# Modulation weights read by TensorE in fp32 as they land, in four column tiles, with the first loads and the DFT put in another order

## The reference, cut to what matters

```
sh_a, sc_a, g_a, sh_m, sc_m, g_m = split(silu(c) @ mod_w[i] + mod_b[i], 6)      # mod_w[i]: 1024 x 6144
h = modulate(x, norm_mix_g[i], sh_a, sc_a)                                      # norm, scale, shift
x = x + g_a * mixer(h)                       # Fourier, differential attention, MLA, Fourier
x = x + g_m * sq_relu_mlp(modulate(x, norm_mlp_g[i], sh_m, sc_m), w1, w2)       # 1024 -> 4096 -> 1024
```

## Time and profile before

| | |
|---|---|
| median of 3 runs | 3569.93 us (3569.45 to 3571.2) |
| the profiled execution | 3565.45 us |
| its span, first to last instruction | 3564.2 us |
| mean granted TensorE clock | 0.956 |
| busy: PE, DVE, ACT, POOL | 3267.6, 1996.8, 1624.1, 1341.1 us |
| moved | 460.01 MB, mean 129 GB/s |

### The profile page before, as it was taken

How to read it: one execution, slowest core, us unless ns; L and a number is a source line. 1 busy time by engine, 2 the same in 40 slices (tenths; PEclk the granted TensorE clock), 3 DMA queues, 4 the chain that set the end, 5 groups by cost and what they waited for, 6 DMA issues and landing times.

```text
span 3564.2 us, 51196 instructions
## 1 busy us (share of the span) xinstructions
PE 3267.6 (92%) x21038; PEld 2848.7 (80%) x21038; DVE 1996.8 (56%) x3159; ACT 1624.1 (46%) x2532; POOL 1341.1 (38%) x542
## 2 busy tenths in 40 slices
PE   4989999897678999979998898999999999999899
PEld 3868888785557888756898897787899987878899
DVE  5465544428855555366665664656546646664565
ACT  4454333325444333355544444555444445555443
POOL 4343344224432444401344333243353442434434
PEclk7999999997779999989999999999999999999999
DMA  6344444322322444411453454233355542434454
GB/s 201 118 130 154 154 154 143 106 83 95 118 95 83 151 148 150 138 42 36 155 189 116 154 179 128 86 107 96 107 168 161 172 133 85 118 95 136 150 179 152
DMA packets 469159, 460.01 MB, mean 129 GB/s; under 512 B 8896, under 2 KB 467520, under 8 KB 468928
## 3 DMA queue, kind: packets, MB, share of 16 engines
q1 hardware_dynamic: 465760, 453.32, 39.9%
q10 hardware_dynamic: 3168, 3.42, 0.3%
HBM read 455.66 MB, written 1.05 MB: 128 GB/s over the span
## 4 chain that ended last, share of the span: by engine, by line
PE 74%; DVE 13%; ACT 7%; issue 3%; POOL 2%; ACTq 0%; DMA 0%; DVEq 0%; POOLq 0%; SPq 0%
PE bank L341 21%; PE bank L342 20%; PE bank L343 20%; ACT wh L289 3%; DVE wl L304 2%; PE bank L382 2%; PE bank L383 2%; POOL wl L316 1%; DVE de L1187 1%; DVE sm L1174 1%; POOL sq L451 1%; PE bank L1328 1%; DVE hl L644 1%; PE bank L1319 1%; DVE sm L1172 1%
## 5 line engine op out<-in xcount | busy, mean ns | idle before, releaser
L316 POOL TENSOR_TENSOR wl<-raw,wh 128x768 fp32r<-128x768 f32 (+4 forms) x432 | 1212.2, 2812 | 2073.9 <-ACT wh L289 2073.9
L289 ACT ACTIVATE wh<-raw 128x2048 fp32r<-128x2048 f32 (+2 forms) x432 | 818.9, 1896 | 474.5 <-PE bank L343 450.3
L304 DVE TENSOR_TENSOR wl<-raw,wh 128x1280 fp32r<-128x1280 f32 (+2 forms) x408 | 679.2, 1665 | 452.3 <-ACT wh L289 451.9
L341 PE MATMUL bank<-nh,wh 128*128 128x272 f32 (+1 forms) x1712 | 510.1, 298 | 23.4 <-DVE nl L1651 22.8
L341 PE MATMUL bank<-xh,wh 128*128 128x512 f32 (+2 forms) x1312 | 462.1, 352 | 45.3 <-ACT xh L499 33.4
L343 PE MATMUL bank<-nh,wl 128*128 128x272 f32 (+1 forms) x1712 | 497.4, 291 | 0.0
L342 PE MATMUL bank<-nl,wh 128*128 128x272 f32 (+1 forms) x1712 | 496.1, 290 | 0.0
L342 PE MATMUL bank<-xl,wh 128*128 128x512 f32 (+2 forms) x1312 | 455.3, 347 | 0.0
L343 PE MATMUL bank<-xh,wl 128*128 128x512 f32 (+2 forms) x1312 | 454.6, 347 | 0.0
L341 PEld LDWEIGHTS bank<-nh,wh 128*128 128x128 f32 x1712 | 330.4, 193 | 40.0 <-issue 37.8
L341 PE MATMUL bank<-hh,wh 128*128 128x512 f32 (+1 forms) x1024 | 348.9, 341 | 3.5 <-DVE X L551 1.9
(11 more groups left out here) (397 smaller groups left out, 6209.2 us busy)
## 6 DMA issues: line engine op xcount, KB each, us to landing
raw<-in_mlp_w SPq DMA_DIRECT2D x128, 1024.0 KB, 5.4
raw<-in_mod_w SPq DMA_DIRECT2D x96, 1024.0 KB, 5.2
raw<-in_w_in SPq DMA_DIRECT2D x60, 1024.0 KB, 5.2
raw<-in_w_mlp_up SPq DMA_DIRECT2D x32, 1024.0 KB, 5.7
raw<-in_w_mlp_down SPq DMA_DIRECT2D x32, 1024.0 KB, 5.1
raw<-in_w_in SPq DMA_DIRECT2D x34, 512.0 KB, 4.6
raw<-in_w_ssd_down SPq DMA_DIRECT2D x16, 1024.0 KB, 5.3
raw<-in_diff_w_qkv SPq DMA_DIRECT2D x12, 1024.0 KB, 5.1
```

The source lines that it names most:

```text
L289: nc.scalar.activation(self.wtile(self.wh, c1), self.wtile(self.raw, c1), AF.Copy).then_inc(*up("act_wh", ("wh", c1)))
L304: nc.vector.tensor_tensor(l, r, h.bitcast(F32), ALU.subtract).then_inc(*up("dve_wl", ("wl_dve", c1)))
L316: nc.gpsimd.tensor_tensor(l, r, h.bitcast(F32), ALU.subtract).then_inc(*up("pool_wl", ("wl_pool", c1)))
L341: nc.tensor.matmul(o, ah, bh, start=first, stop=False)
```

## The change

Modulation chunks are not split any more. TensorE waits for the raw chunk itself and reads it as the moving operand of true fp32 matmuls; `cst` has 32 columns (two used), and row tile k goes into column tile k % 4, output partitions 32 (k % 4) onward, so that eight products with two rounds per column tile make a chunk. Two chunks (even and odd i) share a bank; the copy into `mrow`, the turn and the addition are done once for both. The turn is four fp32 matmuls with `mrow` (128x128) as stationary and `sel` (two columns that add up the four column tiles) as moving operand; VectorE adds once. The banks are 6 and 7 in place of the ring.

Since a modulation chunk stays in `raw` until TensorE has used it, a load waits for `used` of the chunk three before it where that is a modulation chunk. `wh` and `wl` slots and the look-ahead of three now count only the other chunks (`dense`, `nth`). At the start, five more raw buffers lie where `wh` and `wl` will be (EARLY = 8), and four chunks are loaded ahead of the DFT table. The first sum of squares is made by ScalarE and eight matmuls, without GpSimd. The 12 chunks of the Fourier layer are used inside the DFT loop, two behind each of the steps 1 to 6. In the attention two chunks are done behind each even unit, 0 to 22.

```
 def chunks(a):
...
-                if L == 0 and j < 3:
-                    mods(0, 8 + 4 * j, 12 + 4 * j)
+                if L == 0:
+                    mods(0, *((8, 14), (14, 16), (16, 18), (18, 20))[j])
...
-            mods(2, 0, 24, 0)
+            mods(2, 0, 24)
...
     def sp_load(self, upto):
-            if c >= RAWS:
-                SP.wait_ge(*at("wh", c - RAWS))
-                SP.wait_ge(*at("wl_dve", c - RAWS))
-                SP.wait_ge(*at("wl_pool", c - RAWS))
+            if c >= EARLY:
+                prev = c - EARLY if c < EARLY + RAWS else c - RAWS
+                if prev in self.nth:
+                    SP.wait_ge(*at("wh", prev))
+                    SP.wait_ge(*at("wl_dve", prev))
+                    SP.wait_ge(*at("wl_pool", prev))
+                else:
+                    SP.wait_ge(*at("used", prev))
...
+    def split_upto(self, c, ahead):
+        return min(self.nth[c] + ahead, len(self.dense))
+
-    def act_split(self, c):
-        while self.n_act <= min(c + SLOTS - 1, len(self.P) - 1):
-            c1 = self.n_act
+    def act_split(self, c, ahead=SLOTS):
+        while self.n_act < self.split_upto(c, ahead):
+            d, c1 = self.n_act, self.dense[self.n_act]
             ACT.wait_ge(*at("raw", c1))
-            if c1 >= SLOTS:
-                ACT.wait_ge(*at("used", c1 - SLOTS))
+            if d >= SLOTS:
+                ACT.wait_ge(*at("used", self.dense[d - SLOTS]))
+            else:
+                ACT.wait_ge(*at("used", RAWS + 2 * d))
...
-    def pe_mod(self, c, of=RING):
+    def pe_mod(self, c, rows=(6,), cols=(7,)):
-        h, l = self.pe_take(c)
+        PE.wait_ge(*at("raw", c))
         PE.wait_ge(*at("cst"))
-        b = self.pe_bank(of, "mod", L, i)
+        w = self.rawtile(c).rearrange("p (k n) -> p k n", k=8)
+        b = self.place["mod", L, i // 2] if i % 2 else self.pe_bank(rows, "mod", L, i // 2)
         for k in range(8):
-            nc.tensor.matmul(b[:, 0:256], self.cst[:, k, :], h[:, k, :], start=(k == 0), stop=False)
-            ins = nc.tensor.matmul(b[:, 0:256], self.cst[:, k, :], l[:, k, :], start=False, stop=(k == 7))
-        ins.then_inc(*up("pe_acc", ("acc", "mod", L, i), ("used", c)))
-        self.pe_turn()
-        self.turning = L, i, of
+            q = 32 * (k % 4)
+            ins = nc.tensor.matmul(b[q:q + 32, 256 * (i % 2):256 * (i % 2) + 256], self.cst[:, k, :], w[:, k, :], start=(k < 4), stop=(k >= 4))
+        ins.then_inc(*up("pe_acc", ("acc", "mod", L, i // 2), ("used", c)))
+        if i % 2:
+            self.turning = L, i // 2, cols
...
     def pe_turn(self):
-        for u in range(2):
-            ins = nc.tensor.transpose(b[:, 4 * u:4 * u + 4], r[0:4, 128 * u:128 * u + 128], self.ident[0:4, 0:4])
+        for u in range(4):
+            ins = nc.tensor.matmul(b[:, 2 * u:2 * u + 2], self.mrow[h % 2][:, 128 * u:128 * u + 128], self.sel[:], start=True, stop=True)
...
     def act_mod(self, c):
+        if i % 2 == 0:
+            return
+        nc.scalar.activation(self.mrow[h % 2][:], self.place["mod", L, h][:], AF.Copy).then_inc(*up("act_row", ("row", L, h), ("out", "mod", L, h)))
...
     def act_mlp(self, st, T, xs=None, nxt=None):
-            self.act_split(c)
             if p[0] == "mod":
                 self.act_mod(c)
                 c += 1
                 continue
+            self.act_split(c)
...
     def pe_fourier(self, L, S):
+            if L == 0 and 1 <= n <= 6:
+                self.pe_turn()
+                for i in (6 + 2 * n, 7 + 2 * n):
+                    self.pe_mod(self.ix["mod", 0, i])
+        self.pe_turn()
...
     def act_fourier(self, L, S):
+            if L == 0 and 1 <= n <= 6:
+                self.act_mod(self.ix["mod", 0, 7 + 2 * n])
+                if n >= 4:
+                    self.act_split(self.ix["fw", L, n - 4], 1)
...
     def pe_diff(self):
-            if mods and (n > 12 or n in (0, 2, 4, 6, 8, 10, 12)):
+            if mods and n >= 0 and n % 2 == 0:
+                self.pe_mod(mods.pop(0), (7,))
                 self.pe_mod(mods.pop(0), (7,))
...
     def sp(self):
-        self.sp_load(1)
+        self.sp_load(3)
         self.sp_dft(0)
```

More of the change, by code:

```diff
@@ L29 @@
 SLOTS = 3
+EARLY = 8
 RING = (0, 1, 2, 3)
@@ L114, in w, with mods @@
         out.append((name, w3(ap, r0, kt, c0, n), kt, n, share))
-    def mods(layer, lo, hi, share=5):
+    def mods(layer, lo, hi):
         for i in range(lo, hi):
-            w(("mod", layer, i), a["mod_w"][layer], 0, 8, 256 * i, 256, share)
+            w(("mod", layer, i), a["mod_w"][layer], 0, 8, 256 * i, 256)
     mods(0, 0, 8)
@@ L191, in __init__ @@
         self.ix = {p[0]: c for c, p in enumerate(self.P)}
+        self.dense = [c for c, p in enumerate(self.P) if p[0][0] != "mod"]
+        self.nth = {c: d for d, c in enumerate(self.dense)}
         self.loaded = self.n_act = self.n_dve = self.n_pool = 0
@@ L215, in memory @@
         self.wl = [self.mem(f"wl{i}", 2048, F32R, b + 16384 * i + 8192) for i in range(SLOTS)]
+        self.early = [self.mem(f"early{i}", 2048, F32, b + 8192 * i) for i in range(EARLY - RAWS)]
         b += 16384 * SLOTS
@@ L744, in pool_dft, with pe_start_total, square0 @@
                                 ALU.subtract).then_inc(*up("pool_tl", ("tl", L)))
+    def pe_start_total(self, k0):
+        nc, at, up, PE = self.nc, self.T.at, self.T.up, self.PE
+        if k0 >= 8:
+            return
+        if k0 == 0:
+            self.pe_bank((5,), "tot", "mix0")
+        for k in range(k0, k0 + 4):
+            PE.wait_ge(*at("sq", "mix0", k))
+            ins = nc.tensor.matmul(self.place["tot", "mix0"][:], self.ones[:], self.square0(k)[:], start=(k == 0), stop=(k == 7))
+            ins.then_inc(*up("pe_acc", ("square0", k), ("acc", "tot", "mix0")))
+    def square0(self, k):
+        return self.tmp[k] if k < 4 else (self.sq, self.rs, self.rtt, self.tmp[0])[k - 4]
     def pe_fourier(self, L, S):
@@ L879, in dve_fourier @@
                                             ALU.subtract).then_inc(*up("dve_yl", ("yl", L, s, 2 * g + ft), ("out", "fb", L, n - 1, ft)))
+            if L == 0 and 1 <= n <= 6:
+                self.dve_mod(self.ix["mod", 0, 7 + 2 * n])
+                if n >= 4:
+                    self.dve_split(self.ix["fw", L, n - 4], 1)
         for j in range(4):
-            if L == 0 and j < 3:
-                for i in range(8 + 4 * j, 12 + 4 * j):
-                    self.dve_split(self.ix["mod", 0, i])
-                    self.dve_mod(self.ix["mod", 0, i])
             self.dve_split(self.ix["fw", L, j])
@@ L1237, in pool_diff @@
         for j in range(12):
-            self.pool_split(self.ix["qkv", j])
-        for i in range(24):
-            self.pool_split(self.ix["mod", 2, i])
+            self.pool_split(self.ix["qkv", j], min(SLOTS, 12 - j))
         for j in range(4):
```

173 lines of the change are left out of this document (77 added, 96 removed).

## The result

The changed kernel takes **3589.43 us** (median of 4 runs, 3584.13 to 3592.72), the kernel before 3569.69 in the same comparison (4 runs, 3569.3 to 3571.2): ratio 1.0053, 95% interval 1.0036 to 1.0071. It is slower by half a per cent, 20 us; 3540 was forecast. The profiled execution took 3592.72 us for a span of 3591.4.

The account below looks back on a forecast made before the run. TensorE, busy for 92% of the span, was taken to bound the kernel, VectorE being busiest in the attention. The terms -25, +73, +22, -80 and -19 sum to -29 us from 3570: 3541, rounded to 3540, range 3445 to 3610.

Parts of the forecast that it names:

- part 3: Attention: GpSimd's and ScalarE's modulation splits and VectorE's held operations go, turns halve; -80 us, between -45 and -105.
- part 2: MLPs: held raw buffers delay ScalarE's split and row copy, so TensorE waits before the turn; +73 us, plus +22 for the clock.
- the clock after the waits: MLPs: after longer waits modulation matmuls take 0.41 in place of 0.28 us; ten to twelve times about 2 us, +22 us.
- Part 1: MLPs: modulation chunks and turns cost TensorE 1.7 in place of 2.2 us a chunk; 52 chunks, -25 us, between +65 and -35.
- The rival with two tiles at a time: Modulation chunks: column tiles run only two at once, each chunk costs 0.95 us more; +40 us, 3610 us, chance 0.13.
- Sixteen waits: MLPs: TensorE idle before the turn on ScalarE's row copy, 16 times at named places, 2.2 to 7.0 us each.
- the odd chunk before it is free: MLPs: a missing modulation chunk, every seventh place, breaks the chain of waits, so the odd chunk ahead of it has no wait.
- The sign of being right: Attention: no VectorE operation over 2 us and a stage near 162 us would show the forecast right.
- Part 4: Start and layer 0's Fourier part: earlier norm, chunks moved into the DFT loop, two waits; -19 us, between -40 and 0.
- the two waits in the DFT loop: Fourier part: mods 16 and 17 land late behind the load of `fw1`, the same a step later; about 9 us each.
- the row is in time: Rival: the MLP wait before the turn does not come or is short, ScalarE being ahead; -124 us, 3446 us, chance 0.20.
- The attention gives little: Rival: in the attention VectorE's wait for the row copy replaces the held operations; -35 for -80, 3585 us, chance 0.12.

Follow-up runs that it names:

- experiment 1: Changed kernel with weight chunks split two steps ahead, not three, in the two modulated MLPs; 3457.92 us, 0.9694 of the kernel before.
- experiment 4: Kernel before, with GpSimd's low parts of the 24 attention modulation chunks left out and all matmuls kept; 3506.23 us, 0.9830.
- experiment 7: Changed kernel, attention pairs spaced wider, first wo split later: pairs ahead of the values, 3581.18 us; or one chunk per step, 3578.96 us.
- experiment 3: Changed kernel with the Fourier layer's first output weight chunk loaded behind modulation chunks 14 and 15, the others one pair later; 3571.54 us, 1.0012.
- experiment 6: Changed kernel with only four of the eight products of each modulation chunk made in the attention; 3584.13 us, 1.0047 of the kernel before.

## Why the prediction was wrong

The sign was wrong: 29 us of gain were forecast and 27 of loss came, profile against profile (20 in the medians). The time lies in the stated range, 3445 to 3610, and slower had a chance of 0.28, but that range was wide enough for a gain and a loss. The mechanisms that the prediction named were there, save one term of part 3; the terms for the MLPs and for the attention were off by 34 and 18 us, both to the bad side. The prediction was a small difference of large terms. Three steps failed. In part 2 an odd chunk ahead of a gap was taken to be free, and the clock after the waits was put too low; in part 3 ScalarE's splits and the turns were taken to be worth 17 us.

| term | forecast | measured | how |
|---|---|---|---|
| 1, chunks and turns in the MLPs | -25 | -27 | 110.9 to 84.1 us from start to start |
| 2, waits before the turn | +73 | +92.5 | L421 |
| 2, the clock after them | +22 | +35 | wide matmuls +20.7 and +14.4 |
| 3, attention | -80 | -62 | stage |
| 4, start and Fourier | -19 | -18.5 | stage |
| not forecast | 0 | +8 | stages' ends, qkv, rest |

**Part 1 was right**, in the sum. Four column tiles do run at once: a chunk takes 1.07 us, and 28.3 / 28 = 1.01 of TensorE's time, where 0.95 + 0.3 was taken; the 0.3 for entering and leaving was not needed. The rival with two tiles at a time is refuted by this row. Against 16 x 0.24 = 3.8 us one after another that is 3.6 times faster. The turn cost 18.3 / 14 = 1.3 us in the first MLP in place of 0.9, since it came behind a wait at the low clock; with the waits gone (experiment 1) it is 11.5 / 14 = 0.82. The Trainium skill (TensorE: Matmul & The Clock Gate, Part 3, measured speedups) has 2.38 times for three column tiles, from which 1.2 us was estimated; the 1.01 us measured here are nearer to the full four, and they decide.

**Part 2 had the right mechanism and too small a size**, and here the largest part of the error lies: 19.5 us in the waits and 13 in the clock. Sixteen waits were named, and all sixteen are there: the six of `m1` took 7.6 to 8.3 us in place of 7.0 (47.6 in all in place of 42), those of `m2` 2.1 to 2.8 for 2.2 to 2.9, n = 29 5.9 and 5.1 for 5.3. The step that failed is "the odd chunk before it is free", said of the missing M; n = 31, at the end of the list, was put at nothing too. Free it is at n = 12, 19 and 26, but n = 5 waits 3.5 and 3.4 us and n = 31 4.3 and 2.9, 14 us in all. At n = 5 no load is missing: the split at the top of the step finds its chunk. But ScalarE comes to it late. At the top of step 4 it stood for the load behind the even chunk of that step, until 295.89; the two results of step 4, an `m1` chunk, kept it until 303.41, and TensorE had used the chunk of step 5 by 302.3:

```profile
295.89 1.92 ACT L310 ACTIVATE wh<-raw 128x2048 fp32r<-128x2048 f32 x1 [16.54 <-DMA raw<-in_mlp_w]
...
301.27 1.07 PE L407 MATMUL bank<-raw,cst 128*32 128x256 f32 x16
...
303.41 1.91 ACT L310 ACTIVATE wh<-raw 128x2048 fp32r<-128x2048 f32 x1
...
310.84 0.59 ACT L433 ACTIVATE mrow<-bank 128x512 f32<-128x512 f32 x1
...
311.57 1.84 PE L421 MATMUL bank<-sel,mrow 128*128 128x2 f32 x8 [3.53 <-ACT mrow L433]
```

I had counted each odd chunk as if ScalarE began its step on time. It does so at n = 12, 19 and 26, which follow a short `m2` step, and not at n = 5 and 31, which follow a long one (at 31 with the squares). The rows above are all that shows this; no run tries it by itself.

**The clock** was put at some ten to twelve stretches of 2 us, 22 us, and cost 35: a term of the right kind that was sized too small. The price was guessed from one kind of matmul and the longer waits; experiment 1 shows only the total, which goes away with the waits.

**Part 3 had the right cause, and one term that came to nothing.** The 63 us of held VectorE operations are what the stage falls by without GpSimd's (experiment 4), though that it fits to the microsecond is luck, as said there. On top I had put 17 us for ScalarE's 46 us of splits and the turns. The kernel of experiment 4 still has those splits, the 24 turns and TensorE's dearer chunks, and its stage, 234.7 us, is no longer than the changed kernel's 235.8. All that the change takes away beside GpSimd's operations, less what its pairs bring, is worth nothing there. VectorE does not stand 5 us less for the turns, as I had it, but 35.3 us in place of 24.7, and 38.6 in experiment 4. Counted from start to start, TensorE in the changed kernel has 30 us less of chunks than in experiment 4 and 4 less of turns and their waits; but it stands 13 us more before the transposes (21.9 for 8.7) and 12 before the values (19.5 for 7.1), and the scores, values and transposes take 13 us more (88.4 for 75.1), at a clock of 0.77 in place of 0.87. TensorE's saved work comes back as idle time and lower clock. Where the pairs stand costs 9 us of it (experiment 7). That with VectorE free the round trips of a unit through three engines set the stage is what I take from this; no run shows it, and the rest is not taken apart. The sign of being right, a stage near 162 us, was counted from a window of 242 us that ends 10 us before the last `xh`. To the last `xh` it was 252.7 us before and is 190.0 after, 63 less, where 80 were forecast.

**Part 4 was right**: the norm begins at 48.68 for 50 forecast, the two waits in the DFT loop came to 7.5 + 1.0 and 8.2 + 0.8 us for about 9 each, the last group ends at 191.4 for 192, and the cause that was given, the split of the first output weights in SyncE's way, was confirmed by experiment 3.

Of the rivals, "the row is in time" (3446) did not come but is what the design is worth: experiment 1 gives 3458. "The attention gives little" (35 in place of 80, 3585) was true by four tenths: 62 came, and not by the wait that it named, since TensorE waits only 2.0 us for the row copy there. That its time is near the measured one is luck: part 2 made up for the rest.

## What to carry to other kernels

When data is used where it lands, its buffer is held for longer, and the question is which in-order engine asks for the next load of that buffer, and what stands behind it. Here ScalarE prefetched one step further than the buffers allow, and one number, three steps ahead or two, was worth some 130 us, nearly four per cent.

A wait can carry on: at n = 5 ScalarE, late from the step before, made TensorE wait 3.5 us where no load was missing. So a forecast should walk through the places in order and carry the lateness, and where it is the difference of large terms, its chances should say that the sign is open.

In a stage of round trips between small operations, look first for what lengthens the round trip: VectorE operations held by GpSimd were worth 63 of 298 us here. What is taken off an engine beside it must be tried before it is counted: of 12 us of TensorE's 7 showed (experiment 6), and of ScalarE's splits, less what came with them, none.

## What was not expected of the hardware

- The order of column tiles within a chunk makes no difference: 1.07 us with each product on another tile than the last, 1.09 with two in succession on the same.
- 24 GpSimd operations held VectorE for 78 us in five groups, and the stage fell by 63 when they were left out. In the MLPs GpSimd's splits hold `hl<-tmp,hh` too (mean 1297 ns, some 690 where it runs alone; 1308 in experiment 1, where TensorE stands for 1.6 us all the same).
- In the attention TensorE had 30 us less of chunks than in experiment 4 and ran the rest at a lower clock, 0.77 for 0.87, which took 13 us more. That the one brings the other was not tried.
